# A decoder layer on one core: the output projection's last four k blocks as three fp32r products each

## The reference, cut to what matters

```python
o_sb = merge_heads(stick_breaking_attention(...))            # 512 wide, k blocks 0 to 3
o_rg = (jax.nn.gelu(gate_rg) * rg_lru(xc, ...))              # 256 wide, k blocks 4 and 5
o_ca = memory_cross_attention(q_ca, mem, ...)                # 256 wide, k blocks 6 and 7
y = jnp.concatenate([rms_norm(o_sb, g_out_sb), rms_norm(o_rg, g_out_rg), rms_norm(o_ca, g_out_ca)], axis=-1)
x = x + y @ w_out                                            # 256 x 1024 times 1024 x 1024
# then: x = x + moe_ffn(rms_norm(x, g)), 64 experts of width 256, the best 8 per token, and one shared expert
```

## Time and profile before

| | |
|---|---|
| median of three runs | 583.2 us (582.86 to 632.82) |
| the profiled execution | 584.03 us |
| its span, first to last instruction | 582.3 us |
| outside the span | 1.7 us |
| TensorE busy | 552.1 us (95%) |
| VectorE busy | 209.3 us (36%) |
| ScalarE busy | 159.5 us (27%) |
| GpSimd busy | 24.2 us (4%) |
| moved by DMA | 227.51 MB, 391 GB/s mean |
| granted TensorE clock | 0.994 of full speed |

### The profile page before, as it was taken

How to read it: one execution, slowest core, us unless ns; L and a number is a source line. 1 busy time by engine, 2 the same in 40 slices (tenths; PEclk the granted TensorE clock), 3 DMA queues, 4 the chain that set the end, 5 groups by cost and what they waited for, 6 DMA issues and landing times.

```text
span 582.3 us, 8347 instructions
## 1 busy us (share of the span) xinstructions
PE 552.1 (95%) x3164; PEld 307.3 (53%) x3165; DVE 209.3 (36%) x533; ACT 159.5 (27%) x308; POOL 24.2 (4%) x78
## 2 busy tenths in 40 slices
PE   8999999999999999999999989999999989689975
PEld 6988875466444445555455544544544444245332
DVE  2889798684325222220222221111222221221113
ACT  5787366343111122220222221122111212121102
POOL 1006231100000000000000000000000000000000
PEclk9999999999999999999999999999999999898999
DMA  8997469968999999999999999999999999999994
GB/s 318 419 420 298 186 271 424 345 241 314 383 382 423 423 420 421 429 424 423 425 425 424 429 419 426 427 424 426 426 422 427 433 420 427 422 425 424 423 409 184
DMA packets 27929, 227.51 MB, mean 391 GB/s; under 512 B 3312, under 2 KB 3440, under 8 KB 7792
## 3 DMA queue, kind: packets, MB, share of 16 engines
q1 hardware_dynamic: 27600, 226.67, 94.3%
q10 hardware_dynamic: 288, 0.29, 0.1%
HBM read 225.90 MB, written 1.05 MB: 390 GB/s over the span
## 4 chain that ended last, share of the span: by engine, by line
PE 71%; DMA 21%; SPq 4%; DVE 3%; issue 1%; ACT 0%
PE ps L1771 27%; DMA cell_two<-in_w_e 14%; PE ps L1800 10%; PE ps L1729 7%; PE ps L1829 5%; PE ps L1636 5%; DMA cell_three<-in_w_e 4%; PE ps L1532 4%; PE ps L1499 3%; SPq L586 2%; DMA cell_d<-in_w_e 2%; PE ps L1513 2%; SPq L580 1%; PE ps L1791 1%; PE ps L1521 1%
## 5 line engine op out<-in xcount | busy, mean ns | idle before, releaser
L1771 PE MATMUL ps<-cell_two,xg 128*64 128x512 f32 (+2 forms) x624 | 123.5, 611 | 13.1 <-DMA cell_two<-in_w_e 11.4
L1800 PE MATMUL ps<-cell_d,e_hT 128*64 128x512 f32 (+2 forms) x488 | 93.4, 597 | 2.7 <-DVE e_hT L1391 2.7
L1771 PEld LDWEIGHTS ps<-cell_two,xg 128*64 128x64 f32 (+2 forms) x624 | 41.0, 131 | 93.4 <-issue 93.4
L1771 PE MATMUL ps<-cell_gu,xg 128*64 128x512 f32 (+2 forms) x416 | 78.6, 595 | 1.9 <-DMA cell_gu<-in_w_e 1.8
L1388 DVE TENSOR_TENSOR e_h<-e_sg,ps 128x256 f32<-128x256 f32 x28 | 11.8, 421 | 182.2 <-ACT e_sg L906 182.2
L906 ACT ACTIVATE e_sg<-ps 128x256 f32<-128x256 f32 x28 | 10.7, 384 | 204.0 <-PE ps L1771 204.0
L1456 DVE SCALAR_TENSOR_TENSOR ylo<-ps,gslot,yhi 128x512 fp32r<-128x512 f32 (+1 forms) x53 | 39.2, 740 | 73.8 <-ACT yhi L917 73.8
L1729 PE MATMUL ps<-pick,xhi 128*128 128x256 f32 x224 | 58.5, 300 | 0.3 <-DVE pick L1304 0.3
L917 ACT ACTIVATE yhi<-ps,gslot 128x512 fp32r<-128x512 f32 (+1 forms) x53 | 35.9, 679 | 71.6 <-PE ps L1800 70.2
L1729 PE MATMUL ps<-pick,xlo 128*128 128x256 f32 x224 | 54.3, 281 | 0.0
L1729 PEld LDWEIGHTS ps<-pick,xhi 128*128 128x128 f32 x224 | 42.3, 189 | 19.8 <-issue 19.7
(11 more groups left out here) (342 smaller groups left out, 639.0 us busy)
## 6 DMA issues: line engine op xcount, KB each, us to landing
cell_two<-in_w_e SPq DMA_DIRECT2D x39, 2048.0 KB, 28.7
cell_d<-in_w_e SPq DMA_DIRECT2D x59, 1024.0 KB, 26.4
cell_gu<-in_w_e SPq DMA_DIRECT2D x48, 1024.0 KB, 18.6
wo<-in_w_out SPq DMA_DIRECT2D x1, 4096.0 KB, 12.5
wA<-in_w_qk SPq DMA_DIRECT2D x7, 512.0 KB, 10.8
wR<-in_w_rest SPq DMA_DIRECT2D x3, 1024.0 KB, 28.4
cell_three<-in_w_e SPq DMA_DIRECT2D x1, 3072.0 KB, 24.4
wV<-in_w_v SPq DMA_DIRECT2D x1, 2048.0 KB, 18.6
```

The source lines that it names most:

```text
L1771: last = mm(ps[side * w:(side + 1) * w, U, :], rows(k, slice(side * w, (side + 1) * w)), weight[:, k - k0, :], start=k == 0, stop=k == KD - 1)
L1800: last = mm(ps[side * w:(side + 1) * w, Y[half], :], e_hT[:, kk, side * w:(side + 1) * w], n[:, kk, half * 512:(half + 1) * 512], start=kk ...
```

## The change

The last four k blocks (4 to 7) of the output projection are done as three fp32r products each: `yT_hi` by `wo_hi`, `yT_hi` by `wo_lo`, `yT_lo` by `wo_hi`. Pieces 0 to 3 (k 0 to 3) stay float32.

- ScalarE casts the four blocks of `wo` to `wo_hi` (`projection_high`): blocks 0 and 1 in the walk behind the copy "t" of head 6, blocks 2 and 3 behind the first group's root. The gain of a block 4 to 7 is now written rounded to `yT_hi`. The root of group 1 moves behind block 6's square and gain.
- GpSimd subtracts to get `wo_lo` in place of the upper half of `wo` (`projection_low`): 0, 1 and 2 behind the first sums of squares, 3 between the sums of groups 1 and 2.
- VectorE gets `yT_lo` with `rows_low(k)`: 4 and 5 behind `ca_evac(3)`, 6 and 7 behind `mean_square(1)`, ahead of `residual(4)`.
- `wo_hi` takes 16 KB per partition, the ring's cells 9 and 10. `first_cells` is rearranged and SyncE's order of loads changed: `high` of the shared expert is asked for last instead of first, `down 3` earlier, `low 6` and `down 6` later, `low` and `high` of the shared expert after the last projection piece. The planner gives other cells to many of the later loads.

```diff
-    first_cells = [16, 4, 17, 5, 3, CELLS, 1, 6, 2, 7, 8, 9, 10, 11, 18, 12, 13, 14, 20, 0, 19, 15]
+    first_cells = [16, 4, 17, 5, 3, CELLS, 1, 6, 2, 7, 0, 8, 11, 20, 18, 12, 14, 9, 13, 10, 19, 15]
...
+    wo_hi = at("wo_hi", o_ring + 72 * KB, [P, KD // 2, D], F32R)
+    wo_lo = at("wo_lo", o_A + 16 * KB, [P, KD // 2, D], F32R)
...
+    yT_lo = at("yT_lo", r.offset + 4 * KB, [P, KD // 2, SEQ], F32R)
+    yT_hi = at("yT_hi", o_O + 8 * KB, [P, KD // 2, SEQ], F32R)
...
             sp.wait_ge(o_ps, SB_HEADS)
-            load_shared("high")
             load_fixed("low", 3)
             load_fixed("high", 3)
+            load_fixed("down", 3)
             sp.wait_ge(unit_ps, 20)
             load_fixed("low", 4)
             load_fixed("high", 4)
-            load_fixed("down", 3)
             load_fixed("down", 4)
             load_fixed("low", 5)
-            load_fixed("low", 6)
...
             sp.wait_ge(yrg_dve, 2)
-            load_fixed("down", 6)
+            load_fixed("down", 5)
             sp.wait_ge(wo_ps, 4)
-            load_shared("low")
+            load_fixed("low", 6)
             sp.wait_ge(unit_ps, 35)
             load_fixed("down", 2)
             sp.wait_ge(wo_ps, 10)
             load_fixed("high", 6)
+            load_fixed("down", 6)
             sp.wait_ge(wo_ps, len(projections))
-            load_fixed("down", 5)
+            load_shared("low")
+            load_shared("high")
...
+            def projection_low(k):
+
+                pool.wait_ge(whi_act, len(splits) + k + 1)
+                pool.tensor_tensor(wo_lo[:, k, :], wo[:, KD // 2 + k, :], wo_hi[:, k, :].bitcast(F32),
+                                   ALU.subtract).then_inc(wo_lo_pool, 1)
+
+            projection_low(0)
+            projection_low(1)
+            projection_low(2)
             pool.wait_ge(unit_ps, 26)
             for k in (4, 6):
+                if k == 6:
+                    projection_low(3)
                 pool.wait_ge(ysq_act, k + 2)
...
+                dst = yT[:, k, :] if k < KD // 2 else yT_hi[:, k - KD // 2, :]
+                nc.scalar.mul(dst, yT[:, k, :], vec[:, GOUT + k:GOUT + k + 1]).then_inc(yg_act, 1)
+
+            def projection_high(k):
+
+                act.wait_ge(wo_loaded, 16)
+                act.wait_ge(unit_ps, 14)
+                nc.scalar.copy(wo_hi[:, k, :], wo[:, KD // 2 + k, :]).then_inc(whi_act, 1)
...
+            group_root(0)
+            projection_high(2)
+            projection_high(3)
+            for i in range(2):
+                act.wait_ge(yrg_dve, i + 1)
+                square_and_gain(4 + i)
+            act.wait_ge(oca_dve, 1)
+            square_and_gain(6)
+            group_root(1)
+            act.wait_ge(oca_dve, 2)
+            square_and_gain(7)
+            group_root(2)
...
+            def rows_low(k):
+
+                dve.wait_ge(yg_act, k + 1)
+                nc.vector.scalar_tensor_tensor(yT_lo[:, k - KD // 2, :], yT[:, k, :], vec[:, GOUT + k:GOUT + k + 1],
+                                               yT_hi[:, k - KD // 2, :].bitcast(F32), ALU.mult, ALU.subtract).then_inc(alo_dve, 1)
...
+                    if t == 0 and half == 0 and g:
+                        pe.wait_ge(alo_dve, 1 + KD + k + 1 - KD // 2)
+                        pe.wait_ge(wo_lo_pool, k + 1 - KD // 2)
...
+                    for m, (y, w) in enumerate(((yT_hi, wo_hi), (yT_hi, wo_lo), (yT_lo, wo_hi))):
+                        last = mm(ps[:, ACC[2 * t + half], :], y[:, k - KD // 2, rows], w[:, k - KD // 2, c],
+                                  start=k == chunks[0] and m == 0, stop=k == chunks[-1] and m == 2)
```

More of the change, by code:

```diff
@@ L338, in hybrid_decoder_layer @@
             ca_rs_dve, gates_dve, ahi_act, alo_dve, whi_act, wlo_dve, yg_act, ysum_pool, g_rt_act,
+            wo_lo_pool,
         ) = [ctx.enter_context(nc.semaphore(name)) for name in """
@@ L348, in hybrid_decoder_layer @@
             ca_rt_act ca_rs_dve gates_dve ahi_act alo_dve whi_act wlo_dve yg_act ysum_pool g_rt_act
+            wo_lo_pool
         """.split()]
@@ L351, in hybrid_decoder_layer @@
         wA0_half = [ctx.enter_context(nc.semaphore(f"wA0_half{i}")) for i in range(2)]
-        wA_loaded = [ctx.enter_context(nc.semaphore(f"wA_loaded{n}")) for n in range(8)]
+        wA_loaded = [ctx.enter_context(nc.semaphore(f"wA_loaded{n}")) if n else None for n in range(8)]
         wR_loaded = [ctx.enter_context(nc.semaphore(f"wR_loaded{g}")) for g in range(3)]
@@ L783, in square_and_gain @@
                 nc.scalar.activation(y_sq[:, k, :], yT[:, k, :], ACT.Square).then_inc(ysq_act, 1)
-                nc.scalar.mul(yT[:, k, :], yT[:, k, :], vec[:, GOUT + k:GOUT + k + 1]).then_inc(yg_act, 1)
+                dst = yT[:, k, :] if k < KD // 2 else yT_hi[:, k - KD // 2, :]
[4 more added lines that the diff above has]
+                nc.scalar.copy(wo_hi[:, k, :], wo[:, KD // 2 + k, :]).then_inc(whi_act, 1)
             for kind, n in walk:
@@ L814, in _ @@
                     nc.scalar.copy(wT[n % 2][:], ps[:, 6, 0:NZ]).then_inc(wT_act, 1)
+                    if n == SB_HEADS - 2:
+                        projection_high(0)
+                        projection_high(1)
                 elif kind == "ca_norm":
@@ L849, in _, with group_root @@
             nc.scalar.activation(rg_t[:], rg_t[:], ACT.Sqrt, scale=-1.0).then_inc(rg_act, 1)
[L850 to L854, removed]
+            def group_root(g):
                 freed(act, SUMS[g])
                 nc.scalar.activation(g_rs[:, g, :], g_rs[:, g, :], ACT.Sqrt).then_inc(g_rt_act, 1)
+            group_root(0)
[10 more added lines that the diff above has]
+            group_root(2)
             def high_part(t):
@@ L1196, in _ @@
                 nc.vector.tensor_tensor(yT[:, 4 + c, :], rg_g[:, c, :], rg_r[:, c, :], ALU.mult).then_inc(yrg_dve, 1)
+            def rows_low(k):
+                dve.wait_ge(yg_act, k + 1)
+                nc.vector.scalar_tensor_tensor(yT_lo[:, k - KD // 2, :], yT[:, k, :], vec[:, GOUT + k:GOUT + k + 1],
+                                               yT_hi[:, k - KD // 2, :].bitcast(F32), ALU.mult, ALU.subtract).then_inc(alo_dve, 1)
             ca_evac(2)
             ca_evac(3)
+            rows_low(4)
+            rows_low(5)
             ca_result(0)
@@ L1205, in _ @@
             mean_square(1, RG)
+            rows_low(6)
+            rows_low(7)
             residual(4)
@@ L1632, in project @@
                 chunks = ((0, 1, 2, 3), (4, 5), (6, 7))[g]
+                rows, c = slice(t * P, (t + 1) * P), slice(half * 512, (half + 1) * 512)
                 for k in part or chunks:
-                    if t == 0 and half == 0:
+                    if t == 0 and half == 0 and not g:
                         pe.wait_ge(yg_act, k + 1)
-                    last = mm(ps[:, ACC[2 * t + half], :], yT[:, k, t * P:(t + 1) * P],
-                              wo[:, k, half * 512:(half + 1) * 512], start=k == chunks[0], stop=k == chunks[-1])
+                    if t == 0 and half == 0 and g:
+                        pe.wait_ge(alo_dve, 1 + KD + k + 1 - KD // 2)
+                        pe.wait_ge(wo_lo_pool, k + 1 - KD // 2)
+                    if not g:
+                        last = mm(ps[:, ACC[2 * t + half], :], yT[:, k, rows], wo[:, k, c],
+                                  start=k == chunks[0], stop=k == chunks[-1])
+                        continue
+                    for m, (y, w) in enumerate(((yT_hi, wo_hi), (yT_hi, wo_lo), (yT_lo, wo_hi))):
+                        last = mm(ps[:, ACC[2 * t + half], :], y[:, k - KD // 2, rows], w[:, k - KD // 2, c],
+                                  start=k == chunks[0] and m == 0, stop=k == chunks[-1] and m == 2)
                 if k == chunks[-1]:
```

## The result

| | before | after |
|---|---|---|
| median | 583.52 us (582.86 to 632.82, 6 runs) | 592.95 us (590.40 to 594.52, 6 runs) |
| ratio | | 1.0147 (95% interval 1.0128 to 1.0166) |
| profiled execution | 584.03 us | 590.62 us |
| span | 582.3 us | 588.9 us |
| ratio of the same two kernels once more (e11) | | 1.0117 (1.0092 to 1.0143) |

One run before took 632.82 us, the others at most 584.57, and the ratio is that of the others. The change makes the kernel slower: 8.6 us by the first ratio, 6.8 by the second, 6.6 between the two profiled executions. The profiled execution after was the second fastest of its six, so its 6.6 us lie at the low end. 586.7 was forecast, with 589.0 as the upper end.

A forecast was written before the change was run, and what follows sets the result against it. The end was taken as the router's moment plus fixed bytes of expert loads, with VectorE next behind TensorE ahead of it. Holds of 5.3 us on `residual(4)`, less later savings, made +3.5: 583.2 + 3.5 = 586.7 us, range 580.9 to 589.0.

The forecast's parts named there:

- +3.5 us forecast at the router: Net delay at the router: `residual(7)` 4.5 us later, less waits of 1.07 us that VectorE's chain behind it loses.
- The first subtraction runs to 91.4 beside maxima that VectorE reads from PSUM: free.: GpSimd's first subtraction, starting when the sums of squares end at 89.09, was to cost VectorE's maxima nothing.
- rival (c): The lock also catches the maxima's two-element scalings at 89.4 and after: 1.7 us more, 588.4 us; chance 0.12.
- The hold of 1.8 that I put on the first scaling of the probabilities: The second subtraction, running to 93.8, was to shut out VectorE's scaling due at 92.07: +1.8 us.
- The product, "+1.2": The third subtraction, running to 100.5, was to delay VectorE's product, otherwise due at 99.2, by 1.2 us.
- The fourth, "+2.3": The fourth subtraction, between `rows_low(4)` and `rows_low(5)`, was to hold the second up to 108.7: +2.3 us.
- `rows_low`, "0.4 of pace": VectorE's four 128x256 subtractions for `yT_lo` were taken at 0.4 us each, 1.6 us in all.
- The three holds: VectorE delays from GpSimd's subtractions, +1.8, +1.2 and +2.3: 5.3 us on `residual(4)`, 114.2 in place of 108.9.
- Behind it: After `residual(4)`: piece 6 +5.2 us, pieces 6 and 7 save 0.7, VectorE's chain to the last residual loses 1.07 of waits.
- TensorE: 48 fp32r matmuls at 0.229 us replace 14.1 us of float32 ones, 3.1 less; idle about 6 us between 94 and 115.
- ScalarE and the ring, nothing: Four casts of 1.07 us fit in idle gaps; later expert loads stay covered by the queue: both cost nothing.
- (a): Rival: no lock against VectorE, or only short holds; the sum without GpSimd, -1.7 us, gives 581.5 us; chance 0.30.

The follow-up runs named there:

- e11: The changed kernel itself, unaltered, run again against the kernel before; ratio 1.0117.
- e4: Changed kernel with subtractions 0 and 1 on VectorE ahead of the maxima, 2 and 3 on GpSimd behind `rows_low(5)`; ratio to before 1.0043.
- e1: Kernel before with only the new `first_cells` and SyncE load order; 584.15 us for 584.39, ratio 0.9995.
- e2b: Changed kernel without GpSimd's four subtractions, the second product repeating `yT_lo` by `wo_hi`; ratio to before 0.9997.
- e7: Kernel before, float32 throughout, with the changed ring and four GpSimd subtractions whose results nobody uses; ratio to before 1.0083.
- e6: Changed kernel with a GpSimd fill of the same 128x1024 tile in place of each subtraction; ratio to before 1.0006.
- e5: Changed kernel with GpSimd's first two subtractions held back until the four maxima are done; ratio to before 1.0118.
- e3: Changed kernel with each GpSimd subtraction of 1024 columns cut into four of 256; ratio to before 1.0088.
- e8: Changed kernel with all four subtractions on VectorE and none on GpSimd; ratio to before 1.0034.
- e9: Kernel with all four subtractions on VectorE, with piece 5's six matmuls done twice; ratio to before 1.0018.

## Why the prediction was wrong, step by step

The direction, the mechanism and the stretch were right; the holds on VectorE were put too small: +3.5 us forecast at the router, +6.6 measured.

- **"The first subtraction runs to 91.4 beside maxima that VectorE reads from PSUM: free."** This step failed. The maxima themselves were free (0.68 us), the two-element scalings between them were not: 1.84 and 1.50 us more than 0.17. That was rival (c), which I gave 0.12 because they are tiny, and sized at 1.7. What is held does not matter by its size: 0.17 us of work waits for the end of a 2.3 us instruction. The hold of 1.8 that I put on the first scaling of the probabilities did not come, because VectorE was by then past both subtractions' end; so this step is off by 3.34 less 1.8, 1.5 us.
- **The product, "+1.2".** 2.04: the third subtraction, begun at 101.15, let the first product finish and held the next one almost whole. 0.8 more.
- **The fourth, "+2.3".** The pair took 3.26 of pace against 1.17 in e4, where they are free: 2.1. Right.
- **`rows_low`, "0.4 of pace".** 0.585: some 0.55 us more for three. Sized from a product of the same shape.
- The three holds are 7.5 us against 5.3, `rows_low` makes 8.0; `residual(4)` came at 117.17 where 114.2 was forecast, 0.29 of it start-up.
- **Behind it**, residuals 4 to 7 took 3.90 us instead of 5.18, -1.3 where the forecast's +6.0 and +4.5 make -1.5; from there to the last residual 6.68 instead of 7.80, -1.12 for the forecast's -1.07. Right. (The row of 121.15 in the earlier trace rows names VectorE's own fill as the end of its 0.87 us; piece 11's matmuls ended at 121.06 in that trace, so TensorE is the likelier.) From the last residual to the first routed load it is 14.63 us for 14.33 before, and 14.63 to 14.65 in every run with the fp32r form (14.33 in e1 and e7, the float32 ones): 0.3 us that the form costs there and the sum had at nothing. Why stays open.
- **TensorE.** Eighteen matmuls in 4.37 us at full clock, 0.24 each for 0.229. Idle 5.95 us, "about 6" forecast, and that is luck: the delay was 3 us larger, but the low clock stretched twelve matmuls at 113.11 to 4.61 us, 1.8 more than at 0.233 each, and these count as busy. The saving shows only behind `residual(4)`, in the 1.3 and 1.1 us above. The low clock cost next to nothing in this kernel by its rows: the chain goes through the slow matmuls to 118.06, but piece 6 also needed `residual(4)`, which ended at 117.92 and had waited for `rows_low(7)`.
- **ScalarE and the ring, nothing.** Right: the ring by e1; and in e2b, with all casts, the first product starts at 97.25 us, where before has 97.37.
- **(a), -1.7 without any lock.** e2b measures -0.8. Start-up taken off, its `residual(7)` comes level with before where 0.7 earlier was forecast, mostly by `rows_low`; the two waits behind it are gone as forecast (the last residual is 1.1 earlier); and the 0.3 behind that is lost. So even the good case was half of what I gave it.
- **The range** took in rival (c) alone at 588.4, and not (c) together with a product held in full. With 8.0 in place of 5.3 the same sum gives 589.4, and with all that the trace shows (+6.6) 589.8. The first ratio makes 591.8 of 583.2, the second 590.0: all above 589.0. About 2 us of the first are not in its trace.

## What to carry to other kernels

Before giving work to an idle GpSimd, write VectorE's instructions of that stretch beside it and mark those with two SBUF inputs and those that scale from SBUF to SBUF: each of these, down to two elements, may wait for the end of the GpSimd instruction (those with two inputs only where GpSimd reads SBUF), while the reductions, copies and residuals that read PSUM kept their times here. Ask what the engine behind VectorE then does: where a TensorE-bound stretch gets holes, its clock can fall and charge a second time (0.50 and 1.5 us in e6). And a saving on an engine counts only up to the engine next to it: 3.1 us of matmuls were worth 0.8 at the best here (e2b).

## What the runs showed that I had not expected

- A VectorE scaling of 128x2 held for 1.84 us by a GpSimd subtraction and 1.30 by a fill that reads nothing; two of 128x256 held 4.2 us by two subtractions in a row (e5).
- A fill of 128x1024 (0.95 us) beside two-input VectorE instructions costs these nothing (e6), a subtraction of that size (2.35) up to 2.1.
- In e6 the held scaling did not get in between two fills that followed each other; in the changed kernel one did get in between two subtractions.
- Cutting each of GpSimd's subtractions in four lowers the loss by 1.9 of 6.6 us, no more (e3).
- The granted clock fell to 0.50 after TensorE had been busy 1.24 of 2 us and 1.53 of the next 2 (e6), and stayed at 1.00 after 1.25 and 1.88 (e2b). In e8's kernel, where it fell too, six redundant matmuls brought the first routed load forward by 0.9 us (e9).
